# Summing the four convolution tiles on POOL before the sum over the partitions

## The reference, cut to what matters

```python
def layernorm(x, g, b):
    xf = x.astype(jnp.float32)
    mu = jnp.mean(xf, axis=-1, keepdims=True)
    var = jnp.mean(jnp.square(xf - mu), axis=-1, keepdims=True)
    y = (xf - mu) * lax.rsqrt(var + EPS)
    return (y * g.astype(jnp.float32) + b.astype(jnp.float32)).astype(x.dtype)

def conformer_conv(u, ug, w_dw, b_dw, ln_g, ln_b, w_pw):
    a = u * jax.nn.sigmoid(ug)
    y = lax.conv_general_dilated(a, w_dw[:, None, :].astype(a.dtype), ...) + b_dw.astype(a.dtype)
    y = layernorm(y, ln_g, ln_b)
    y = jax.nn.silu(y)
    return jnp.einsum('btc,cd->btd', y, w_pw)

merged = jax.nn.sigmoid(ga) * a_out + jax.nn.sigmoid(gb) * c_out
```

## Time and profile before

| | |
|---|---|
| median of 3 runs | 2289.99 us (2288.27 to 2291.29) |
| profiled execution | 2288.2 us, of which the span is 2286.4 us |
| PE busy | 2242.4 us (98%) |
| DVE busy | 1286.8 us (56%) |
| ACT busy | 960.6 us (42%) |
| POOL busy | 212.6 us (9%) |
| granted clock of PE | 0.999 of full speed |

### The profile page before, as it was taken

How to read it: one execution, slowest core, us unless ns; L and a number is a source line. 1 busy time by engine, 2 the same in 40 slices (tenths; PEclk the granted TensorE clock), 3 DMA queues, 4 the chain that set the end, 5 groups by cost and what they waited for, 6 DMA issues and landing times.

```text
span 2286.4 us, 30902 instructions
## 1 busy us (share of the span) xinstructions
PE 2242.4 (98%) x11476; PEld 1822.5 (80%) x11476; DVE 1286.8 (56%) x1931; ACT 960.6 (42%) x1580; POOL 212.6 (9%) x154
## 2 busy tenths in 40 slices
PE   7999999999999999999999999999999999999999
PEld 6887898887888898876778888888886668888887
DVE  6467656365444227998664444333989664544433
ACT  5545454354333224226954333222323963433322
POOL 3000031020000001021031000001012022000001
PEclk9999999999999999999999999999999999999999
DMA  5221033013222222221122222232321122322232
GB/s 206 106 79 56 20 129 131 36 56 129 92 92 100 103 102 91 80 90 39 55 75 92 92 101 101 92 105 91 111 74 56 38 75 74 112 108 92 92 111 73
DMA packets 29492, 203.33 MB, mean 89 GB/s; under 512 B 3264, under 2 KB 3904, under 8 KB 5696
## 3 DMA queue, kind: packets, MB, share of 16 engines
q1 hardware_dynamic: 28224, 197.11, 24.4%
q10 hardware_dynamic: 1152, 4.69, 0.6%
HBM read 199.69 MB, written 2.10 MB: 88 GB/s over the span
## 4 chain that ended last, share of the span: by engine, by line
PE 86%; DVE 6%; issue 4%; ACT 2%; POOL 1%; DVEq 0%; DMA 0%; ACTq 0%; POOLq 0%
PE bank L403 25%; PE bank L405 24%; PE bank L404 24%; DVE cy L2293 1%; PE bank L973 1%; PE bank L2068 1%; PE bank L2042 1%; PE bank L2055 1%; PE bank L944 1%; PE bank L961 1%; PE bank L1942 1%; PE bank L1538 1%; PE bank L1515 1%; PE bank L2045 1%; PE bank L502 1%
## 5 line engine op out<-in xcount | busy, mean ns | idle before, releaser
L403 PE MATMUL bank<-x_hi,w_hi 128*128 128x512 f32 (+1 forms) x2032 | 791.2, 389 | 22.5 <-DVE x_lo L394 10.1
L405 PE MATMUL bank<-x_hi,w_lo 128*128 128x512 f32 (+1 forms) x2032 | 775.9, 382 | 0.0
L404 PE MATMUL bank<-x_lo,w_hi 128*128 128x512 f32 (+1 forms) x2032 | 775.0, 381 | 0.0
L290 ACT ACTIVATE w_hi<-w_raw 128x2048 fp32r<-128x2048 f32 x167 | 319.7, 1917 | 609.6 <-PE bank L405 607.7
L294 DVE TENSOR_TENSOR w_lo<-w_raw,w_hi 128x2048 fp32r<-128x2048 f32 x167 | 385.1, 2307 | 324.9 <-ACT w_hi L290 324.9
L403 PEld LDWEIGHTS bank<-x_hi,w_hi 128*128 128x128 f32 x2032 | 382.6, 188 | 100.3 <-issue 20.4
L405 PEld LDWEIGHTS bank<-x_hi,w_lo 128*128 128x128 f32 x2032 | 382.5, 188 | 75.3
L404 PEld LDWEIGHTS bank<-x_lo,w_hi 128*128 128x128 f32 x2032 | 383.1, 189 | 72.6 <-issue 2.9
L403 PE MATMUL bank<-f_hi,w_hi 128*128 128x512 f32 (+1 forms) x572 | 215.2, 376 | 0.0
L404 PE MATMUL bank<-f_lo,w_hi 128*128 128x512 f32 (+1 forms) x572 | 215.0, 376 | 0.0
L405 PE MATMUL bank<-f_hi,w_lo 128*128 128x512 f32 (+1 forms) x572 | 215.0, 376 | 0.0
(11 more groups left out here) (351 smaller groups left out, 2706.8 us busy)
## 6 DMA issues: line engine op xcount, KB each, us to landing
w_raw<-w_d SPq DMA_DIRECT2D x184, 1024.0 KB, 4.8
h<-x_d ACTq DMA_DIRECT2D x4, 512.0 KB, 8.7
out_d<-h SPq DMA_DIRECT2D x4, 512.0 KB, 6.2
tab<-rope_d ACTq DMA_DIRECT2D x2, 640.0 KB, 3.9
w_raw<-w_d SPq DMA_DIRECT2D x2, 512.0 KB, 5.7
memT<-mem_d ACTq DMA_DIRECT2D x1, 1024.0 KB, 4.8
stage<-cmask_d SPq DMA_DIRECT2D x1, 384.0 KB, 6.8
pos_i<-pos_d SPq DMA_DIRECT2D x1, 256.0 KB, 6.2
```

What stands on the lines that cost most here:

```text
L290: act.activation(w_hi[:, u.slot, :], w_raw[:, u.slot, :], ACT.Copy).then_inc(hi_ready, 1)
L403: pe.matmul(dst, wh[:, k, cols], hi[:, kx_, at:at + width], start=start, stop=False)
L404: pe.matmul(dst, wh[:, k, cols], lo[:, kx_, at:at + width], start=False, stop=False)
L405: return pe.matmul(dst, wl[:, k, cols], hi[:, kx_, at:at + width], start=False, stop=stop)
```

## The change

POOL gets three more adds per layer, placed behind the rope products and ahead of the adds of squares. The first adds tile 1 to tile 0 into `conv_squares(0)` as soon as half 0 of the taps is counted, the second adds tile 3 to tile 2 into `conv_squares(2)` when all taps are, the third adds these two. PE waits for the third add, not for the taps, and makes one matmul with the ones instead of four. The counts of `ln_add` go from three to six per layer.

```diff
                 if t == AT_SUM:
-                    pe.wait_ge(l_tap, L * 4 * TAPS + 4 * TAPS)
+                    pe.wait_ge(ln_add, L * 6 + 3)
                     pe.wait_ge(l_gs, L * 16 + 11)
-                    for m in range(4):
-                        mm = pe.matmul(bank[:, 5, :], ones[:, :], cy[:, m, :], start=(m == 0), stop=(m == 3))
-                    mm.then_inc(ln_sum, 1)
+                    pe.matmul(bank[:, 5, :], ones[:, :], conv_squares(0), start=True, stop=True).then_inc(ln_sum, 1)
                 if t == AT_SS:
-                    pe.wait_ge(ln_add, L * 3 + 3)
+                    pe.wait_ge(ln_add, L * 6 + 6)
...
                     pool.tensor_tensor(lcos[:, t % 2, :], lq[:, rope_at(t), :], cos_q[:, :] if t else cos2, ALU.mult).then_inc(q_cos, 1)
+                for half in range(2):
+                    pool.wait_ge(l_tap, L * 4 * TAPS + (half + 1) * 2 * TAPS)
+                    pool.tensor_tensor(conv_squares(2 * half), cy[:, 2 * half, :], cy[:, 2 * half + 1, :], ALU.add).then_inc(ln_add, 1)
+                pool.wait_ge(ln_add, L * 6 + 2)
+                pool.tensor_tensor(conv_squares(0), conv_squares(0), conv_squares(2), ALU.add).then_inc(ln_add, 1)
                 for n, (a_, b_) in enumerate(((0, 1), (2, 3), (0, 2))):
                     pool.wait_ge(ln_sq, L * 4 + max(a_, b_) + 1)
                     if n == 2:
-                        pool.wait_ge(ln_add, L * 3 + 2)
+                        pool.wait_ge(ln_add, L * 6 + 5)
```

## The result

The changed kernel took 2297.45 us (median of 9 runs, 2294.74 to 2299.56); the kernel before took 2289.99 (median of 9, 2288.07 to 2291.66). The ratio is 1.0035, with a 95% interval of 1.0026 to 1.0043: slower by some 7.5 to 8 us. The forecast was slower by 5.2. The profiled execution took 2299.56 us, its span is 2297.7, and the granted clock 0.994 where before it was 0.999.

What follows compares the result with a forecast made beforehand. DVE and ACT were taken to pace the attention stage, PE having slack. Delays of 1.01 + 0.63 + 0.98 = 2.62 us per layer, handed on as 2.6, make 5.2 in all: 2293.4 profiled, 2295.2 median, range 2291.0 to 2298.0.

Steps and rivals of the forecast that it cites:

- The sum of the adds: The three POOL adds hold up DVE's two-operand work on the path by 2.62 us per layer, bounds 2.42 and 2.82.
- one tiny operation would get through: In the 0.08 us gap between second and third add, one or two of DVE's small operations get through.
- the adds hide: Rival: the POOL adds run without touching DVE; gain 0 to 0.47 us per layer, 2289.1 to 2290.0; chance 0.12.
- only the taps pay: Rival: tiny operations slip between second and third add, only the first add costs, 2.0 us in all, 2292.0; chance 0.09.
- dearer: Rival: second and third add last 1.73 us each; 7.8 us slower in all, 2297.8; chance 0.08.
- The wait that changes: At step 3 PE waits for the third add instead of the last tap; DVE reaches the mean 2.15 us late.
- PE's new wait costs nothing: PE's wait for the third add is free, as the scores behind it need ACT's exponentials, moved from 1054.96 to 1057.6.
- What is late next: Behind the mean, POOL's first add of squares costs DVE 0.44 us more; ACT hands on 2.6 us per layer.
- The collision: The first add of squares runs behind L769 and holds up the centring at 1064.19 by 1.02 us instead.
- It gains nothing by itself: Taking six of eight matmul records, 2.58 us per layer, off PE's sum over the partitions wins no time.
- the 1.11 us of PE's slack at 1083.89: PE's wait at the transposes of 1083.89 was taken as 1.11 us to spare, so ACT's lateness of 2.6 us counts.
- The forecast's own sign: In the profile after, PE's transposes of 1062.65 would come at 1065.2 and those of 1083.89 at 1086.5.

Runs made afterwards that it cites:

- after_again: The changed kernel run once more, unaltered, for the spread of its two layers; 2295.93 us, ratio 1.0032 to the kernel before.
- busy_both: The changed kernel plus three dummy matmuls ahead of PE's wait for the third add and two ahead of step 5's transposes; 2293.70 us, ratio 1.0018.
- one_add: The kernel before with only the first POOL add, beside the last taps; PE sums three tiles; 2291.46 us, ratio 1.0011.
- one_add_early: As one_add, but the POOL add stands ahead of the rope products, in the input projection; 2291.21 us, ratio 1.0007.
- one_tile_busy: one_tile plus two dummy matmuls ahead of the transposes of step 5; 2288.22 us, ratio 0.9996.
- early_busy: one_add_early plus two dummy matmuls ahead of the transposes of step 5; 2287.68 us, ratio 0.9995.
- before_again: The kernel before run once more, unaltered, for the spread of its two layers; 2286.75 us in one execution.
- after: The changed kernel itself, in its first comparison with the kernel before; 2297.45 us, ratio 1.0035.
- keep_busy: The changed kernel with three dummy matmuls ahead of PE's wait for the third add; 2294.94 us, ratio 1.0024.
- one_tile: The kernel before with PE summing only the first tile, the other three left out of the mean, no POOL adds; 2292.14 us, ratio 1.0009.

## Why the prediction was right or wrong

**The sum of the adds: right.** Forecast were 1.01 on the taps, 0.63 on L2356 and 0.98 on L2363, in all 2.62. Measured, in the order of the new lines: 3.10 - 2.07 = 1.03; 0.75 - 0.16 = 0.59; 1.19 - 0.16 = 1.03; in all 2.65. ACT's exponentials of job 2 start 14.01 us behind the last rope product, before 11.39: 2.62 later. The first add took 1.83 us and not 1.09, as it had itself to wait for the tap beside it, but that cost DVE no more than forecast. That one tiny operation would get through was right too. The rivals "the adds hide", "only the taps pay" and "dearer" fall by these rows.

**The wait that changes: its place right, its price wrong.** DVE no longer waits at the mean and is 17.00 - 14.95 = 2.05 us late (forecast 2.15). PE waits 1.50 us for POOL's third add, and its following scores indeed wait for ACT by a further 0.22 us, as forecast. But "PE's new wait costs nothing" counted only what is queued behind it, not what it does to PE's clock.

**What is late next: half right.** The collision moved from L769 to the centring as forecast, for 2.19 - 1.28 = 0.91 us instead of the full 1.02, so 0.33 more than before instead of 0.44. Not foreseen was that the later adds of squares then miss L2370 and L773, whose 0.74 and 0.49 us fall away (at full clock, in after_again, one of them then holds L2354 up by 0.38). ACT kept most of the 2.6 all the same. What reaches the end of the span at full clock is 2.40 us per layer (busy_both, after_again) against 2.6 forecast.

**The step that failed** is "It gains nothing by itself, since PE next has to wait for ACT and DVE", and with it the 1.11 us of PE's slack at 1083.89. I had read PE's waits as room, free to grow, and had put the price of a longer wait at nothing. But behind longer waits the granted clock fell, and with the waits filled it did not. PE, relieved of 2.58 us per layer and held back by ACT's lateness, stood idle for 1.50 and then 0.6 to 2.3 us, and did the next 3 to 10 us of work at 1.2 GHz. There the matmuls of L403 to L405 follow each other 0.43 us apart instead of 0.23, and that is more than the slack holds. The forecast's own sign shows the place: the transposes that were to move from 1062.65 to 1065.2 came at 1068.28, which is 1065.26 without the 3.02 us lost earlier, and those that were to come at 1086.5 came at 1091.27, or 1088.25, so 1.75 late. It cost 1.4 to 2.0 us per layer in three of the four layers seen (44.69, 44.84 and 45.23 against 43.27) and nothing in the fourth. The mean of the four is 44.51, which is 3.64 over 40.87, or 7.3 us for two layers. The medians differ by 7.5 in the first comparison and by 6.2 in that of after_again. The four layers come from the longest of nine executions and the shortest of six, so that 7.3 comes so close to 7.5 is partly luck.

The sum of the forecast was thus too small by one missing term. The size that I gave, 5.2, is what busy_both shows: 4.8 by the spans, 1.0018 (1.0009 to 1.0028) by the device times, that is 2 to 6 us. The ratio puts the changed kernel at the upper end of the range that I had given, 2298.0.

**Open** is what exactly decides whether the clock falls. one_add waited 2.07 and 2.08 us and kept it in both layers, one_add_early waited 2.09 and 2.08 and lost it in both, after_again waited 2.28 and kept it in one layer. Shown is only that it stayed up in all six layers of the three kernels in which the waits were filled (busy_both, one_tile_busy, early_busy), and in those of the kernel before, whose longest wait there is 1.23 us. Short falls of the clock elsewhere differ between executions of one kernel: near 225 us in before and none in before_again, near 225, 525 and 875 in after, and near 300 and 525 in after_again. They were not pursued.

## What to carry to other kernels

Before moving work to an idle engine, look at what its port or memory shares with the engine on the path: here an add on POOL, which was 9% busy, stopped even a two-element operation of DVE until the add had ended. And before relieving an engine that isn't the bound, ask what it does with the time: here longer waits of TensorE let its granted clock fall, and matmuls behind them then followed each other 0.43 us apart instead of 0.23. When a time agrees with a theory, check the span in the trace as well, and ask which execution was traced: keep_busy had the expected median, and its trace did not show the expected mechanism.

## What the runs showed of the hardware that was not expected

- Taking 2.58 us of matmuls off TensorE per layer made a layer 1.2 to 1.3 us longer (one_tile), and giving it 1.7 us of useless ones back made it 1.4 to 1.6 us shorter (one_tile_busy).
- At the lower clock a matmul of 128x512 of L403 to L405 is 0.63 us long at 0.43 spacing, at the higher one 0.39 at 0.23. Those with the matrix of ones (L2105) are 0.43 apart at the higher clock already.
- The same wait in the same program doesn't always bring the clock down: 2.28 us in the first layer of after_again kept it, 2.27 in the second didn't.
- A POOL memset of 128x512 takes 0.52 us and left the DVE operations beside it at their length; a POOL add of the same tile takes 1.09 to 1.29 us alone and 1.5 to 2.1 when a DVE operation is under way. It holds DVE's next operation on two SBUF operands until it has ended, for 0.4 to 1.1 us, whatever the size of that operation. DVE operations that read PSUM kept their 0.68 us beside it.
